# Expert stage: products with v summed over eight key blocks in PSUM instead of four, ten places for coefficients, rings of four rows, and a gate tensor stored pair by pair

## The reference

```python
cid = (i1[..., :, None] * PEER_N_KEYS + i2[..., None, :])        # expert = 128 * key one + key two
sc, pos = lax.top_k(cand, PEER_TOPK)                             # 16 experts for each of 8 heads
g = jax.nn.softmax(sc, axis=-1)
u = jnp.take(peer_u, eid, axis=0)
act = jax.nn.gelu(jnp.einsum('cd,chkd->chk', xc, u), approximate=False)
vv = jnp.take(peer_v, eid, axis=0)
return jnp.einsum('chk,chkd->cd', (g * act), vv)
```

## Time and profile before

| | |
|---|---|
| median of three executions | 4499.35 us |
| profiled execution, its own time | 4500.66 us |
| its span, first to last instruction | 4499.1 us |
| mean granted TensorE clock | 0.925 |
| VectorE busy | 3031.3 us (67% of the span) |
| TensorE busy | 3781.7 us (84%) |
| GpSimd busy | 1700.7 us (38%) |
| DMA queue q0, indirect rows and GpSimd's | 561.32 MB, 33.4% of 16 engines |
| DMA queue q1, SyncE's | 409.15 MB, 26.2% |

### The profile page before, as it was taken

The page is one execution under the profiler, slowest core; times in us unless marked ns, Lnnn a source line. Parts: engine busy times, 40 slices in busy tenths (PEclk is TensorE's granted clock), DMA queues, the critical chain, the costliest instruction groups (busy, mean ns, idle before and its releaser), DMA issues. The chain is left out here.

```text
span 4499.1 us, 64773 instructions
## 1 busy us (share of the span) xinstructions
PE 3781.7 (84%) x24917; PEld 3550.5 (79%) x24917; DVE 3031.3 (67%) x5889; ACT 1175.7 (26%) x2134; POOL 1700.7 (38%) x1197
## 2 busy tenths in 40 slices
PE   7999997599998897970674788988888888888887
PEld 7898895499998876870564788888888888888886
DVE  3434433222222344998895899989998999989996
ACT  1313313111111022432892122212222222222221
POOL 0000000000000033775105666667666666666750
PEclk9999998799999998885896899999999999999998
DMA  3122122844443331000248999999999999999994
GB/s 118 37 73 64 26 69 99 307 168 176 163 167 130 127 126 46 28 10 0 113 187 320 350 355 359 356 356 356 354 359 346 367 354 354 361 348 367 353 326 161
DMA packets 434860, 982.93 MB, mean 218 GB/s; under 512 B 48893, under 2 KB 226429, under 8 KB 431522
## 3 DMA queue, kind: packets, MB, share of 16 engines
q0 software_dynamic: 153744, 561.32, 33.4%
q1 hardware_dynamic: 278466, 409.15, 26.2%
q10 hardware_dynamic: 2384, 8.91, 0.5%
HBM read 901.73 MB, written 131.28 MB: 230 GB/s over the span
## 5 line engine op out<-in xcount | busy, mean ns | idle before, releaser
L1920 POOL DMA_INDIRECT u_row<-in_peer_u_dram,eid x512 | 783.6, 1531 | 705.6 <-DVE dots L1979 421.5
L59 PE MATMUL e_ps<-coef_h,v_h 128*128 128x288 f32 x2048 | 660.8, 323 | 245.0 <-DVE v_l L1948 201.2
L59 PE MATMUL e_ps<-hBh,u_h 128*128 128x288 f32 x2048 | 607.3, 297 | 61.7 <-DVE u_l L1941 61.7
L1995 DVE SCALAR_TENSOR_TENSOR f_row<-v_row,g_coef,f_row 128x1024 f32<-128x1024 f32 x508 | 650.6, 1281 | 4.6 <-DMA v_row<-in_peer_v_dram,eid 4.1
L59 PEld LDWEIGHTS e_ps<-coef_h,v_h 128*128 128x128 f32 x2048 | 414.5, 202 | 299.7 <-DVE v_l L1948 247.5
L1926 POOL DMA_INDIRECT v_row<-in_peer_v_dram,eid x512 | 569.6, 1113 | 197.9 <-issue 154.3
L60 PE MATMUL e_ps<-coef_l,v_h 128*128 128x288 f32 x2048 | 634.3, 310 | 0.0
L61 PE MATMUL e_ps<-coef_h,v_l 128*128 128x288 f32 x2048 | 631.9, 309 | 0.0
L1979 DVE CUSTOM_DVE_ANT_0 u_row<-u_row,h_row 128x1024 f32<-128x1024 f32 x512 | 621.0, 1214 | 7.7 <-DMA u_row<-in_peer_u_dram,eid 7.7
L61 PE MATMUL e_ps<-hBh,u_l 128*128 128x288 f32 x2048 | 607.1, 296 | 0.0
L60 PE MATMUL e_ps<-hBl,u_h 128*128 128x288 f32 x2048 | 606.8, 296 | 0.0
(11 more groups left out here) (290 smaller groups left out, 7979.0 us busy)
## 6 DMA issues: line engine op xcount, KB each, us to landing
u_raw<-in_peer_uT_dram SPq DMA_DIRECT2D x128, 512.0 KB, 9.0
v_raw<-in_peer_vQ_dram SPq DMA_DIRECT2D x256, 256.0 KB, 7.7
s_g<-gate_block SPq DMA_DIRECT2D x9, 4096.0 KB, 11.7
x_gate<-s_g SPq DMA_DIRECT2D x64, 576.0 KB
out_o_kv_sample_dram<-in_cache_kv_w_dram SPq DMA_DIRECT2D x32, 1016.0 KB, 7.6
c_raw<-in_conv_tiles_dram SPq DMA_DIRECT2D x40, 512.0 KB, 3.5
w_raw<-in_w_in_dram SPq DMA_DIRECT2D x96, 192.0 KB, 3.7
cache_v<-in_cache_vS_dram SPq DMA_DIRECT2D x8, 2304.0 KB
```

What stands on the lines that cost most here:

```text
L59: pe.matmul(out, lh, rh, start=first, stop=False)
L1920: pool.indirect_dma_start(urow[:, r % RING], None, io["peer_u"][0], bass.IndirectOffsetOnAxis(ap=eid[:, r:r + 1], axis=0)).then_inc(urow_i ...
L1995: dve.scalar_tensor_tensor(out=f, in0=vrow[:, r % RING], scalar=coef[:, s % 2, x:x + 1], in1=f, op0=ALU.mult, op1=ALU.add).then_inc(weighe ...
```

## The change

The group is now g, of eight key blocks (GE = 8, 16 groups). A values phase has 16 calls `values(g, m)`: m // 2 is the piece d of output columns, m % 2 the half of the group. Both halves are summed in the same PSUM banks, so `add` is called once for two calls, 128 times in place of 256; the number of matmuls and of loads stays. Phases of new blocks have eight blocks. The 32 rows of a group are dealt out as before: one row pair to a values call, two to a new block. CS becomes 10. Since SBUF is limited, RING becomes 4. `s_g` is stored as (pair, partition, token block, two keys x 64 tokens): the store of a block has runs of 512 B (64 for each of 128 partitions) where it had one of 32 KB for each partition, and the load of a pair has one run of 4608 B for each partition where it had nine of 512 B. `load_h` and `store_f` move from the end of a turn to behind its second new block.

```diff
@@ build_gates, sync @@
-                sp.dma_start(io["s_g"][b].rearrange("p i t -> p (i t)"),
-                             blk[:, b % 2].rearrange("p i t -> p (i t)")).then_inc(blk_out[b % 2], 16)
+                sp.dma_start(io["s_g"][:, :, b].rearrange("i p n -> p i n"),
+                             blk[:, b % 2].rearrange("p (i w) t -> p i (w t)", w=2)).then_inc(blk_out[b % 2], 16)
@@ experts @@
-    NQ = KEYS // 4
+    GE = 8
+    NGE = KEYS // GE
+    NSL = 2 * KD
-    CS = 6
+    CS = GE + 2
-    RING = 6
+    RING = 4
-        g_view = io["s_g"].rearrange("b p (i w) t -> i p b (w t)", w=2)
+        g_view = io["s_g"].rearrange("i p b n -> i p (b n)")
@@ sync @@
-                sp.dma_start(vraw[:, n % VR], v_view[q, d]).then_inc(v_in[n % VR], 16)
+                sp.dma_start(vraw[:, n % VR], v_view[2 * g + m % 2, m // 2]).then_inc(v_in[n % VR], 16)
+            for g in range(-1, NGE):
+                if g >= 0:
+                    for m in range(VR, NSL):
+                        load_v(g, m)
+                for j in range(GE):
+                    e = GE * g + GE + 2 + j
                     load_u(e + 2)
                     if j % 2 == 0:
                         load_gate(e // 2 + 1)
-                    load_v(q + 1, j)
+                        load_v(g + 1, j // 2)
+                    t, at = divmod(g + 1, NGE // GTILES)
+                    if j == 1 and at == 0 and 1 <= t < GTILES:
+                        if t < GTILES - 1:
+                            load_h(t + 1)
+                        store_f(t - 1)
@@ scalar @@
-                    act.wait_ge(o_ready, KD * ((e - CS) // 4 + 1))
+                    act.wait_ge(o_ready, NSL * ((e - CS) // GE + 1))
...
@@ vector @@
-            def add(q, d):
-                n = q * KD + d
+            def add(g, d):
+                n = g * KD + d
-                dve.wait_ge(o_ready, n + 1)
-                if q == 0:
+                dve.wait_ge(o_ready, 2 * n + 2)
+                if g == 0:
...
+            for g in range(-1, NGE):
+                if g >= 0:
+                    for m in range(NSL):
+                        if m >= 2:
+                            split_v(g, m)
+                            if m % 2 == 0:
+                                add(g, m // 2 - 1)
+                        row(4 * g + 4 + m // HB, m % HB)
+                    add(g, KD - 1)
+                for j in range(GE):
+                    e = GE * g + GE + 2 + j
+                    row(4 * g + 6 + j // 4, 2 * (j % 4))
                     if e <= KEYS:
                         coef_rest(e - 1)
                     if e < KEYS:
                         coefs(e)
                     split_u(e + 2)
+                    row(4 * g + 6 + j // 4, 2 * (j % 4) + 1)
+                    if j >= GE - 2:
+                        split_v(g + 1, j - (GE - 2))
@@ tensor @@
+            def values(g, m):
+                n, d, half = g * NSL + m, g * KD + m // 2, m % 2
+                if m == 0:
+                    pe.wait_ge(c_done, GE * (g + 1))
                 pe.wait_ge(v_lo, n + 1)
+                if half == 0 and d >= 2:
+                    pe.wait_ge(o_added, d - 1)
                 for y in range(2):
                     for b in range(4):
+                        s, cols = (GE * g + 4 * half + b) % CS, slice(y * CW, (y + 1) * CW)
+                        o = split3(pe, ps[:, 4 + 2 * (d % 2) + y, :CW], vh[:, n % 2, b * P:(b + 1) * P],
+                                   vl[:, n % 2, b * P:(b + 1) * P], ch[:, s, cols], cl[:, s, cols],
+                                   half == 0 and b == 0, half == 1 and b == 3)
+                o.then_inc(o_ready, 1)
@@ program @@
-    scratch("s_g", (TB // GB, P, KEYS, GB))
+    scratch("s_g", (KEYS // 2, P, TB // GB, 2 * GB))
```

More of the change, by code:

```diff
@@ L1813, in load_gate, with load_v @@
                     sp.wait_ge(c_full, 2 * p - 2)
-                sp.dma_start(gate[:, p % 2].rearrange("p b w t -> p b (w t)"), g_view[p]).then_inc(gate_in[p % 2], 16)
-            def load_v(q, d):
-                if q >= NQ:
+                sp.dma_start(gate[:, p % 2].rearrange("p b w t -> p (b w t)"), g_view[p]).then_inc(gate_in[p % 2], 16)
+            def load_v(g, m):
+                if g >= NGE:
                     return
-                n = q * KD + d
+                n = g * NSL + m
                 if n >= VR:
                     sp.wait_ge(v_lo, n - VR + 1)
-                sp.dma_start(vraw[:, n % VR], v_view[q, d]).then_inc(v_in[n % VR], 16)
+                sp.dma_start(vraw[:, n % VR], v_view[2 * g + m % 2, m // 2]).then_inc(v_in[n % VR], 16)
             load_u(0)
@@ L1869, in coef_hi, with split_v @@
                 if e >= CS:
-                    act.wait_ge(o_ready, KD * ((e - CS) // 4 + 1))
+                    act.wait_ge(o_ready, NSL * ((e - CS) // GE + 1))
                 act.activation(ch[:, e % CS], tmp[:, e % 2], ACT.Copy).then_inc(c_hi, 1)
-            def split_v(q, d):
-                if q >= NQ:
+            def split_v(g, m):
+                if g >= NGE:
                     return
-                n = q * KD + d
+                n = g * NSL + m
                 act.wait_ge(v_in[n % VR], 16 * (n // VR + 1))
@@ L1897, in _ @@
             coef_hi(0)
[L1898 to L1904, removed]
+            for g in range(-1, NGE):
+                if g >= 0:
+                    gelu_rows(4 * g + 3)
+                    for m in range(2, NSL):
+                        split_v(g, m)
+                        if m == 9:
+                            gelu_rows(4 * g + 4)
+                for j in range(GE):
+                    e = GE * g + GE + 2 + j
                     if e <= KEYS:
@@ L1909, in _ @@
                     split_u(e + 2)
[L1910 to L1913, removed]
+                    if j % 4 == 1:
+                        gelu_rows(4 * g + 5 + j // 4)
+                    if j >= GE - 2:
+                        split_v(g + 1, j - (GE - 2))
         @block.gpsimd
@@ L2040, in _ @@
                     split_u(e + 2)
-                    row(2 * q + 5, 2 * j + 1)
-                    if j >= 2:
-                        split_v(q + 1, j - 2)
+                    row(4 * g + 6 + j // 4, 2 * (j % 4) + 1)
+                    if j >= GE - 2:
+                        split_v(g + 1, j - (GE - 2))
         @block.tensor
@@ L2057, in activations @@
                 m.then_inc(a_ready, 1)
[L2059 to L2062, removed]
+            def values(g, m):
+                n, d, half = g * NSL + m, g * KD + m // 2, m % 2
+                if m == 0:
+                    pe.wait_ge(c_done, GE * (g + 1))
                 pe.wait_ge(v_lo, n + 1)
-                if n >= 2:
-                    pe.wait_ge(o_added, n - 1)
+                if half == 0 and d >= 2:
+                    pe.wait_ge(o_added, d - 1)
                 for y in range(2):
                     for b in range(4):
[L2068 to L2071, removed]
+                        s, cols = (GE * g + 4 * half + b) % CS, slice(y * CW, (y + 1) * CW)
[3 more added lines that the diff above has]
+                o.then_inc(o_ready, 1)
             activations(0)
             activations(1)
[L2075 to L2081, removed]
+            for g in range(-1, NGE):
+                if g >= 0:
+                    for m in range(NSL):
+                        values(g, m)
+                for j in range(GE):
+                    if GE * g + GE + 2 + j < KEYS:
+                        activations(GE * g + GE + 2 + j)
 def ln2_out(nc, io, k):
```

1 line of the change is left out of this document (removed).

## The result

The changed kernel takes 4385.09 us in the median of four executions (4381.8 to 4387.77), the kernel before 4500.6 us beside it (4495.51 to 4504.25). The profiled execution has a span of 4385.2 us (before 4499.1), clock 0.928. Of all executions reported here one, of the kernel before with a ring of four (6799.99 us, clock 0.832), was disturbed and is left out.

The account below looks back on a forecast made before the run. VectorE was taken as the slower engine inside a phase, with TensorE's turn at changes to new blocks. Terms -74 + 10 - 21 - 7 + 3 + 20 = -69 us on 4500.7 gave 4432, as median 4430 us; range 4400 to 4482.

Parts of the forecast that it names:

- The steady part: Expert stage, 15 full groups: 119.06 us each against 124.0 for two old patterns, one phase change fewer, -74 us.
- wait before adds: VectorE before an add: waits for PSUM rise from one of 0.43 us a pattern to 75 us in all.
- V + 63.09: Group timing on VectorE: the next x_tmp product comes 63.09 us after the start of the values phase.
- The end: End of the expert stage: 16 values calls left and no activation, 50.8 us against 72.0, -21 us.
- the last phase: Last new-block phase: six real blocks instead of eight, fewer splits, coefficient operations and products, -7 us.
- Ring of four: Row slots: a slot needs 10.3 us of the 14.5 available; a late row costs its full lateness.
- DMA pressure: New-block phases: 22.8 MB take 58.9 us against 55.97, about half hidden, 1.3 x 15 = +20 us (bounds 0 and 87).
- Rival A: Whole expert stage: DMA engines are the bound already, share 0.97; kernel at 4455 to 4497 us, chance 0.22.
- the start: First new-block phase: eight blocks where four were, 4 x (7.19 - 4.70) = +10 us, range 2 to 18.
- the gate loads: Loads of s_g ahead of u: 128 runs of 4608 B replace 1152 of 512 B; no gain, no stall.
- the gate stores: Stores of s_g in 512 B runs at 348 GB/s: last one lands 2.9 us later, +3 us.
- rival D: Values phases: add wait of 0.67 us doesn't come about, up to 70 us more saved; below 4403 us, chance 0.05.

## Why the prediction was off, point by point

**Right.** The steady part, by its own steps: step length 7.24 us, wait before adds 75 against 74.3, V + 63.09 against 63.17, -74 against -71.4. The claim that the 128 adds turn into waiting almost whole: putting them back costs 13 us. (That the waits sum to 75 is partly luck, as said above.) The end (-21, was -23.1) and the last phase (-7, was -6.5). Ring of four: enough, and three not.

**Wrong: "I take 1.3 x 15 = +20 us"** for DMA pressure. It measured 0, its own lower bound. The step failed in two places. It took it that a phase of new blocks must move 22.8 MB of the 44.3 in its 56 us, and priced that against the rates. The phase in the profile above moved 372 GB/s x 56.10 us = 20.9 MB and the values phase behind it 373 x 63.16 = 23.6: the transfers spread evenly over the group, and VectorE waited for none. And it took 369 GB/s at share 1.00 as near a ceiling; the runs at 387 and 390 GB/s show that it was none. Rival A did not come about. The Trainium skill's limit behind it ("DMA: Bandwidth & Descriptors", Specifications), 358 GB/s, is refuted for this core by the same rows. The Trainium skill gives a reason on another page ("Perfetto Trace Analysis", Roofline): a core whose pair is idle may take more, up to some 120% of that figure. 390 is 109%, which agrees; what the pair's other core did, no run here shows.

**Wrong: the start, "+10 us".** The four blocks more are there, but from the first fetch (2390.77, was 2382.99) to V it is 107.4 us, 6.7 less than before, so about 17 us were gained against the step's +10. The step priced new blocks by the steady state and left out that the stage's start was full of waits: VectorE stood still for 55.2 of the first 114 us (43.2 for u, 7.7 and 4.1 for rows, 0.2 for PSUM), of which the earlier trace rows shows the 7.7. In the changed kernel it is 44.7, so 10.5 of the 17 are waits that went. The layout alone and the ring alone each take the 8.68 us wait away; how the 17 divide in the changed kernel was not tried.

**Wrong: the gate loads, "I count no gain, but no stall either".** No stall is right, and no gain is not: 14 us in the kernel before. More telling is what the count of nothing hid. The part had named the place (u behind the gate, 17.7 us to land) and the danger of eight blocks in a row; priced by taking the layout out, it is 92 us. Without it the change would have gained some 20 us in place of 115.

**Mis-sized: the gate stores, +3.** They land in 16.4 us, 4.7 more than before. The row it went by (348 GB/s) was too kind: 4.19 MB in 16.4 - 2.5 us are 302 GB/s. By the Trainium skill ("DMA: Bandwidth & Descriptors", Specifications), which puts line rate at 512 B, this term would be 0; the trace does not agree, by those 4.7 us.

**Missing: the stalls around f_row's store, -13.2.** The earlier trace rows is a pattern without one, and the sum scaled it by 15. A view of where the x_tmp waits stand over the whole stage would have shown three patterns of 65 to 68 us; the diff moves `store_f`, which was the hint.

The terms at fault, 20 + 13.2 + 12 for start and stores, make up the 45 us by which the sum missed; all three erred the same way. The 4403 below which rival D began was passed, but not by D's mechanism: the add wait came about in full, and the time fell into D's band by the three terms above. D's price was sound all the same: 70 forecast, 65.5 measured when the add was moved.

## What to carry to other kernels

Before a pattern from the middle of a stage is multiplied, list its period over the whole stage; the odd ones out are terms of their own. A load of many small runs costs first those who stand behind it in its queue: move it to another queue, or lay it out in long runs, and price it by the longest stretch in which the load behind it is needed at once. Price a DMA load over the time in which requests may slide, not over the phase in which they are asked for. Where work is removed beside a wait of another engine, ask what the wait becomes; here an add asked for one step later was worth five times the 128 adds removed.

## What the runs showed of the hardware that was not expected

- A DMA share of 0.97 at 354 GB/s is not a full engine: the same loads ran at 387 GB/s with share 1.00 and at 390 with 1.01. A share near 1 did not tell how much room was left.
- 576 KB in 1152 runs of 512 B held up a 512 KB load behind it in the same queue to 17.9 us; from another queue the same runs held up nothing that can be measured (4387 against 4385 us).
- Stores of 4 MB in 512 B runs landed in 16.4 us, in 32 KB runs in 11.7.
- More places for rows made the start of the stage slower: four beat six by 10 us there. That fetches in flight hold up u is likely, and not shown by itself.
